# Half of an even chunk's output products moved behind the odd chunk's state product, and one block of an inverse emptied first

## The reference

```
def step(S, inp):
    rt, wt, kt, vt, at, bt = inp
    sa = jnp.einsum('bhk,bhkv->bhv', at, S)
    S = wt[..., None] * S + bt[..., None] * sa[:, :, None, :] + kt[..., None] * vt[:, :, None, :]
    return S, jnp.einsum('bhk,bhkv->bhv', rt, S)
```

```
A = L + jnp.eye(c, dtype=L.dtype)
sol = lax.linalg.triangular_solve(A, rhs, left_side=True, lower=True, unit_diagonal=True)
...
def step(S, inp):
    u_i, w_i, qk_i, qin_i, kout_i, cd_i = inp
    u = u_i - jnp.einsum('bhik,bhkv->bhiv', w_i, S)
    o = jnp.einsum('bhik,bhkv->bhiv', qin_i, S) + jnp.einsum('bhij,bhjv->bhiv', qk_i, u)
    S = S * cd_i[..., None, None] + jnp.einsum('bhjk,bhjv->bhkv', kout_i, u)
    return S, o
```

## Time and profile before

| | us |
|---|---|
| median of three runs | 2399.49 |
| lowest and highest of them | 2397.66, 2406.66 |
| the profiled execution | 2394.43 |
| its span, first to last instruction | 2392.7 |
| TensorE matmuls busy | 2268.9 (95% of the span) |
| TensorE weight loads busy | 2106.5 (88%) |
| VectorE busy | 1041.6 (44%) |
| ScalarE busy | 691.6 (29%) |
| GpSimd busy | 987.5 (41%) |
| mean granted clock of TensorE | 0.973 of full |

### The profile page before, as it was taken

One profiled execution on the slowest core, in us unless ns is written; L12 is line 12 of the kernel. 1 busy time (PEld: TensorE's weight loads), 2 busy tenths in 40 slices (PEclk: granted clock), 3 DMA queues, 4 the chain that ended last, 5 costly groups with the idle time before them and its releaser, 6 DMA issues. The chain is left out here.

```text
span 2392.7 us, 47012 instructions
## 1 busy us (share of the span) xinstructions
PE 2268.9 (95%) x20560; PEld 2106.5 (88%) x20560; DVE 1041.6 (44%) x1520; ACT 691.6 (29%) x885; POOL 987.5 (41%) x1166
## 2 busy tenths in 40 slices
PE   6989988999999999999989899799899999999997
PEld 3978977988889999999978699679888899999997
DVE  4174766674553512111133756766564444121112
ACT  3435221311323322222234352232121333222221
POOL 1532421352544545554544243124434554555553
PEclk8999989899999999999999999999999999999999
DMA  7332121111333243322233322211123232222222
GB/s 282 126 132 81 63 99 64 45 63 45 129 116 112 70 139 130 106 95 89 89 137 134 119 78 79 71 66 63 45 99 115 99 116 70 93 93 89 89 93 77
DMA packets 68460, 233.41 MB, mean 98 GB/s; under 512 B 10784, under 2 KB 11296, under 8 KB 67872
## 3 DMA queue, kind: packets, MB, share of 16 engines
q1 hardware_dynamic: 61344, 214.88, 25.9%
q10 hardware_dynamic: 6912, 15.53, 1.8%
HBM read 219.03 MB, written 11.35 MB: 96 GB/s over the span
## 5 line engine op out<-in xcount | busy, mean ns | idle before, releaser
L753 POOL TENSOR_TENSOR ring_lo<-ring,w_hi 128x256 fp32r<-128x256 f32 x1104 | 887.4, 834 | 1111.7 <-ACT w_hi L1461 1055.9
L828 PE MATMUL gm<-H_hi,ring_lo 128*128 128x260 f32 x3328 | 697.0, 291 | 11.0 <-POOL ring_lo L753 4.4
L828 PE MATMUL gm<-H_lo,w_hi 128*128 128x260 f32 x3328 | 685.7, 287 | 0.0
L828 PE MATMUL gm<-H_hi,w_hi 128*128 128x260 f32 x3328 | 681.8, 286 | 1.3 <-issue 1.3
L828 PEld LDWEIGHTS gm<-H_hi,ring_lo 128*128 128x128 f32 x3328 | 522.5, 191 | 46.0 <-issue 13.7
L828 PEld LDWEIGHTS gm<-H_lo,w_hi 128*128 128x128 f32 x3328 | 519.8, 190 | 6.9 <-issue 5.1
L828 PEld LDWEIGHTS gm<-H_hi,w_hi 128*128 128x128 f32 x3328 | 518.9, 190 | 7.0 <-issue 5.9
L1461 ACT ACTIVATE w_hi<-ring 128x1024 fp32r<-128x1024 f32 x256 | 270.3, 1056 | 454.1 <-PE gm L828 174.7
L1373 PE MATMUL gm<-AF_hi,ring_lo 128*128 128x260 f32 x704 | 142.1, 283 | 2.2 <-DVE AF_lo L2504 2.2
L2509 DVE TENSOR_TENSOR AT<-gm,GT 128x520 f32<-128x520 f32 x44 | 30.8, 700 | 255.3 <-ACT GT L1768 255.3
L1373 PE MATMUL gm<-AF_hi,w_hi 128*128 128x260 f32 x704 | 141.5, 282 | 0.0
(11 more groups left out here) (399 smaller groups left out, 2810.8 us busy)
## 6 DMA issues: line engine op xcount, KB each, us to landing
ring<-wall SPq DMA_DIRECT2D x372, 512.0 KB, 3.3
WB<-wbranch SPq DMA_DIRECT2D x32, 256.0 KB, 3.8
xsave<-X SPq DMA_DIRECT2D x2, 2080.0 KB, 12.8
X<-xsave ACTq DMA_DIRECT2D x8, 520.0 KB, 5.4
arena<-states ACTq DMA_DIRECT2D x8, 512.0 KB, 4.4
sst<-arena ACTq DMA_DIRECT2D x8, 512.0 KB, 2.7
X<-xt SPq DMA_DIRECT2D x1, 2080.0 KB, 12.1
y<-H SPq DMA_DIRECT2D x4, 520.0 KB, 2.7
```

What stands on the lines that cost most here:

```text
L753: ins = pool.tensor_tensor(ring_lo[:, SLOT[i], k], ring[:, SLOT[i], k], hi[:, k].bitcast(F32), ALU.subtract)
L828: ins = pe.matmul(out[:, hf, 0:HALF], w[a][:, k, :], src[b][:, k, HALF * hf:HALF * (hf + 1)], start=first and a == "lo", stop=last and a == b)
```

## The change

Two things are changed, for the second and the third mixer, in both layers. First, in an even chunk only the first half of the output products (t = 0) is issued in its place. The second half (t = 1) is kept as a function in `late_outputs` and issued in the odd chunk, right behind its state product and that product's signal; the signal to ACT that the even chunk's outputs are complete moves with it. Second, after the inverse's first products DVE empties the block for TOP first, then the two for MT, and signals the TOP block and one MT block by a semaphore each; TensorE waits for that second signal before the product that reads MT.

```
@@ inverse, TensorE
                     operands(sem=operands_a)
+                    pe.wait_ge(operands_v, count.next(operands_v))
                     for u in range(8):
                         ins = pe.matmul(mx[top, 0, HD * u:HD * (u + 1)], PRODUCT[low, u, :], MT[low, u, low],
@@ chunk, TensorE
+                late_outputs = []
 ...
                         ins.then_inc(mix_done_v, 1)
+                        while late_outputs:
+                            late_outputs.pop()()
                         if c == 2:
                             sample_sums(TB[n], (0,))
 ...
-                    for t in range(2):
+                    def outputs(t, last):
                         for tt, e, u, f in heads:
 ...
                         ins = pe.matmul(mx[:, 1, P128 * t:P128 * (t + 1)], state[:, t, :], qin[:, t, cs], start=False,
                                         stop=True, skip_group_check=True)
-                    ins.then_inc(mix_done_a, 1)
+                        if last:
+                            ins.then_inc(mix_done_a, 1)
+
+                    outputs(0, False)
+                    if solved and c % 2 == 0:
+                        late_outputs.append(lambda: outputs(1, True))
+                    else:
+                        outputs(1, True)
@@ inverse, VectorE
-                    for a in (0, 2 * BLK):
-                        r = slice(a, a + BLK)
-                        issue(ts(MT[r, :, a + BLK:a + 2 * BLK], mx[r, 1, 0:8 * BLK].rearrange("p (u i) -> p u i", u=8),
-                                 -1.0, None, MUL))
                     r = slice(BLK, 2 * BLK)
                     step(ts(TOP[r, :, 0:BLK], mx[r, 2, 0:8 * BLK].rearrange("p (u i) -> p u i", u=8), -1.0, None, MUL),
                          operands_v)
+                    for a in (2 * BLK, 0):
+                        r = slice(a, a + BLK)
+                        (step if a else issue)(ts(MT[r, :, a + BLK:a + 2 * BLK], mx[r, 1, 0:8 * BLK].rearrange(
+                            "p (u i) -> p u i", u=8), -1.0, None, MUL), operands_v if a else vector_step)
```

## The result

Twelve runs of each kernel on one chip: before 2397.24 us (median, 2388.82 to 2406.66), after 2384.56 us (2375.25 to 2394.94). The ratio is 0.9944 [0.9924, 0.9965]. The same kernel once more, beside 35 runs of before (2398.11), took 2392.69 us: 0.9976 [0.9956, 0.9996]. So the change makes the kernel faster, by 0.2 to 0.6%, 5 to 13 us.

What follows compares the result with a forecast made beforehand. TensorE, busy for 95% of the span, was taken as the bound, so only its idle time could move. Terms 0.80 + 0.54 + 1.60 - 2 x 0.18 = 2.58 us gave 2396.9 us, range 2389 to 2404.

Steps and rivals of the forecast that it cites:

- The sum of the waits: TensorE waits in the second and third mixers: 0.80 + 0.54 + 1.60 - 2 x 0.18 = 2.58 us saved.
- layer 1's pair: Second mixer's first pair, layer 1: old wait and lost overlap go, a new 0.21 us wait comes; 0.54 us saved.
- the block product: L1096, third mixer's second pair, both layers: needed block emptied first, 0.80 us saved at each, 1.60 us together.
- the sample sums: L1111, third mixer's second pair, even chunk: a new wait of 0.18 us, once per layer.
- layer 0's pair: Second mixer's first pair, layer 0: moved half covers the odd chunk's 0.59 us wait at L1137; 0.80 us saved.
- The rivals on waits: Saved time returns at the next unmoved wait, 2399.5 us, chance 0.20; lost weight-tile cover costs at most about 1 us per layer.
- The rule on weight loads that are pulled ahead: Before L1137: if loads already ran during the wait, 0.19 us per place isn't won, 0.38 us less.
- rivals two and three: From second mixer's first pair: layer 1 loses the clock, 2400.6 us, chance 0.12; or layer 0 keeps it, 2393.3, 0.13.
- either layer may fall in any run: Second mixer's first pair: the clock observation runs on its own time, so either layer may drop to the lower level.
- none of the rivals reaches 12 us: Whole kernel: a measurement can tell about 0.5%, 12 us, from no change; the largest rival effect is 6.2 us.
- rival three: Second mixer's first pair, layer 0: the higher clock is kept, 3.65 us more gained, 2393.3 us; chance 0.13.
- The offset of 5 us: Whole kernel: the median of the runs lies 5.06 us above the profiled run; added to 2391.85 for the forecast.

Runs made afterwards that it cites:

- e8: Kernel before with only the second mixer's half of the outputs moved: 2392.87 us, 0.9980 of before.
- e1: Kernel before, unchanged, run again as a control: 2394.19 us, 0.9984 of before.
- e9: Changed kernel with dummy matmuls in four short waits of the second mixer's first pair: 2377.81 us, 0.9916 of before.
- e10: Kernel before with dummy matmuls in five short waits of the second mixer's first pair: 2387.74 us, 0.9960 of before.
- e17: The same kernel as e9, run again: 2379.66 us, 0.9918 of before.
- e12: Changed kernel with dummies in the second mixer's first pair and six in the weight-tile wait: 2380.24 us, 0.9920 of before.
- e13: Kernel before with dummies in the second mixer's first pair and six in the weight-tile wait: 2388.95 us, 0.9952 of before.
- e15: e10 plus only the inverse's TOP block emptied first: 2383.52 us, 0.9934 of before, -4.2 us against e10.
- e18: e10 plus the second mixer's moved half and the TOP block emptied first: 2380.95 us, 0.9924 of before.
- e14: e10 plus only the second mixer's moved half: 2386.23 us, 0.9940 of before, -1.5 us against e10.
- e2: Kernel before with only the moved half of the outputs, in both mixers: 2390.79 us, 0.9963 of before.
- e5: The changed kernel, unaltered, run again: 2392.69 us, 0.9976 of before.
- e4: Kernel before with only the third mixer's half of the outputs moved: 2397.33 us, 0.9986 of before.
- e16: e10 plus only the third mixer's moved half: 2388.00 us, 0.9955 of before, +0.3 us against e10.
- e11: Kernel before with six dummy matmuls in the wait for a weight tile's second half: 2401.93 us, 1.0012 of before.
- e6: Changed kernel with 28 for 22 dummy matmuls at the third mixer's opening: 2393.18 us, 0.9973 of before.
- e7: Kernel before with 30 for 22 dummy matmuls at the third mixer's opening: 2403.66 us, 1.0025 of before.

## Why the prediction was wrong

**The sum of the waits was right.** Forecast 2.58 us; in the profiles TensorE is out of work for 3.0 us less, and at equal clock after lies 3.1 us (+- 0.4) below before. Each part came out near its own term (-1.2, -2.2, +0.3 at equal clock for 0.98, 1.6 and 0.36, each +- 0.5); e8's -0.4 for 1.34 is the one further off. Of the six places, five (layer 1's pair, the block product and the sample sums in both layers) showed the predicted rows to within 0.05 us. At the sixth, layer 0's pair, the wait went too, but the stretch ran at the lower clock and its state product took 3.51 us where it had taken 2.04, so nothing was won there in that one profile.

**The rivals on waits did not happen.** No weight tile of the third mixer's first pair waits for GpSimd. The profile after lists two waits of 0.15 us for a half tile, at 509.62 and 1677.04, which before's views don't list; but before has the same gaps at 512.30 and 1686.74, and that is another stage. The rule on weight loads that are pulled ahead (the Trainium skill, "TensorE: Matmul & The Clock Gate", its table of specifications) would have made the sum 0.38 us smaller; the weight-load queue's waits went with the matmuls' (8 events to 4 at L1142), so no run here shows it.

**What failed is the step on the clock**, in two sentences of the rivals. First, rivals two and three allowed the clock one place, the second mixer's first pair, and one price, 3.65 us either way. The pair does swing: 0.77 and 0.94 in two profiles of before (e1's is the second), 0.80 and 0.94 in two of after. But 0.17 of 60 us, at twice, are 20 us at the lower level, up to 10 us of TensorE's time, not 3.65. And of the falls that stayed away some lie elsewhere, at 449 and 517, where nothing was moved, and others at L1096, in the third mixer. Second, "either layer may fall in any run" took the swing as evenly spread between the kernels. It isn't: the 24 runs of after have a mean clock of 0.9742, the 117 of before 0.9698 and the 12 of its control 0.9724. That is 3 to 8 us by the slope, and 5.3 us where the swing was taken out. So the sentence that none of the rivals reaches 12 us rested on a bound read from a single profile. The mechanism of rival three, fewer gaps keep the clock up, points the right way; its place and its size were wrong. In the terms of the sum, the block first was priced at 1.60 us, its two waits, and their effect on the clock at nothing, without a reason given; with the pair filled it gave 4.2 and 5.3 us.

The offset of 5 us between the profiled run and the median was the same mistake. It was carried over as a constant, while it is a draw of the clock (0.973 in the profiled run). How far the first series lies below the range is such a draw too: the second, at 2392.69, would have been in it.

**What stays open.** That the change raises the mean clock is shown (e9, e10, e17, and e12 and e13 beside them), and that the block first has a part in it (e15 against e10, e18 against e14); for the second mixer's half the clock points the same way, but the time doesn't exceed its waits clearly. For the block the falls behind L1096 are the likely way. For the half the way is not known. My first theory was that it raises the clock behind the second mixer, because profiles with it (e2, e5, e8, e9) had 6.8 us at the lower level there and no fall at the tile wait, and those without (e1, e4, e10) had 10.2 us and a fall. e14 and e18 have the half, and 10.2 us and a fall, and e18 is 7 us faster than e10 all the same; e17, the same program as e9, has 10.2 us and a fall in layer 1; and e15 and e16, without the half, have no fall at the tile wait. My second, that the single falls there carry the price, found no support in e11 and e13: the falls went, the time stayed. A third, that it hangs on the moment of arrival, had none from e6 and e7, where a shift changed the pattern but not the clock. A record of the clock over many runs of one kernel, where I have one profile of each, would be needed to say more.

## What to carry to other kernels

Where TensorE is busy all the time, split a difference of two profiles into busy time and the rest before looking for waits: the same matmuls at less busy time is clock. Compare kernels at equal granted clock, from many runs, before crediting an edit with a few tenths of a per cent, and give the clock its own term in a forecast, at every wait that the change takes away, with bounds from several profiles or, where there is only one, wide ones. And where sparse small matmuls wait four times for half a microsecond with no other work, try dummies in those waits: it was worth 9 us here, three times what the change's own waits were.

## What the runs showed of the hardware

- 0.001 of mean granted clock is worth 1.76 us in a kernel of 2400 us (299 runs, scatter 1.8 us), about three quarters of the 2.4 us that 0.001 of the time would be.
- One program, before, had mean clocks of 0.9688 and 0.9724 in two series of 35 and 12 runs side by side: 6 us.
- Behind waits of 0.58 to 0.74 us among small matmuls, four or five in some 20 us, 17 to 24 us at the lower level followed in at least one layer in ten of eleven profiles; with dummies in them in none of nine. The Trainium skill, "TensorE: Matmul & The Clock Gate" (Part 1), says that activity releases the fast clock; the filled pair agrees (0.91 to 0.94 in 320 to 380 in all nine profiles, 0.74 to 0.94 without).
- A single wait of 0.74 us ahead of L1096 was followed by 6.8 us at the lower level at 8 of 22 places; where the wait was gone, at 0 of 18.
- A wait of 1.73 us was followed by a fall in before, and one of 1.76 us at the same place wasn't in after: the length of the last wait alone doesn't decide.
